# Expert rows added to gathered residual rows per block, in place of a scratch of expert rows and a combine pass

## The reference

```
h = rms_norm(x, g_norm_ffn) * (1 + sc_m) + sh_m
top-1 of 4 groups, then top-2 of the 8 experts inside it      # 2 rows of 32 experts per token
hid = silu(xblk @ w_gate[e]) * (xblk @ w_up[e])               # 1024 -> 256
y[token] += (hid @ w_down[e]) * weight                        # 256 -> 1024
x = x + gt_m * y                                              # gt_m: one row for the prompt, one for the sample
```

## Time and profile before

| what | us |
|---|---|
| median of 3 runs (lowest to highest) | 1254.57 (1252.77 to 1256.62) |
| the profiled execution's own time | 1249.39 |
| its span | 1247.6 |
| TensorE busy in the span | 1070.9 |
| DVE busy | 554.3 |
| ACT busy | 252.5 |
| POOL busy | 186.9 |
| DMA, mean over the span | 200 GB/s |

### The profile page before, as it was taken

One profiled execution on the slowest core, in us unless ns is written; L12 is line 12 of the kernel. 1 busy time (PEld: TensorE's weight loads), 2 busy tenths in 40 slices (PEclk: granted clock), 3 DMA queues, 4 the chain that ended last, 5 costly groups with the idle time before them and its releaser, 6 DMA issues. The chain is left out here.

```text
span 1247.6 us, 13856 instructions
## 1 busy us (share of the span) xinstructions
PE 1070.9 (86%) x4732; PEld 690.1 (55%) x4732; DVE 554.3 (44%) x1110; ACT 252.5 (20%) x595; POOL 186.9 (15%) x267
## 2 busy tenths in 40 slices
PE   4699999999298889989999994399999999999920
PEld 1245555544255455657666753377777777777610
DVE  2345556554363555566575736511222121222147
ACT  1132232222222222332223201011111111111100
POOL 1122222222501101110110000110110011011032
PEclk9799999999677999999999985599999999999975
DMA  8985555441331122221120105649999999999857
GB/s 316 335 304 195 190 189 188 171 154 44 116 88 59 33 78 76 77 93 35 59 74 4 51 34 222 250 155 363 361 375 368 359 371 374 360 363 369 303 193 262
DMA packets 66860, 249.94 MB, mean 200 GB/s; under 512 B 11555, under 2 KB 15286, under 8 KB 51062
## 3 DMA queue, kind: packets, MB, share of 16 engines
q1 hardware_dynamic: 56208, 219.72, 47.5%
q0 software_dynamic: 7216, 26.22, 6.0%
q10 hardware_dynamic: 3382, 3.32, 0.8%
HBM read 195.58 MB, written 53.65 MB: 200 GB/s over the span
## 5 line engine op out<-in xcount | busy, mean ns | idle before, releaser
L903 PE MATMUL bank<-W_in,hT 128*128 128x512 f32 (+3 forms) x432 | 181.3, 573 | 3.4 <-ACTq L1295 3.4
L1061 PE MATMUL bank<-W_out,mT 128*128 128x512 f32 (+1 forms) x288 | 139.7, 618 | 2.9 <-DVEq L1487 2.9
L903 PEld LDWEIGHTS bank<-W_in,hT 128*128 128x128 f32 (+1 forms) x432 | 79.7, 187 | 94.6 <-issue 89.0
L1178 PE MATMUL bank<-WG,xT 128*128 128x256 f32 x528 | 121.3, 383 | 2.4 <-ACT xT L1435 1.9
L1196 PE MATMUL bank<-WD,hidT 128*128 128x512 f32 x264 | 119.0, 593 | 1.6 <-DVE hidT L1961 1.6
L1180 PE MATMUL bank<-WU,xT 128*128 128x256 f32 x528 | 119.3, 379 | 0.0
L1953 DVE TENSOR_TENSOR hid<-sg,bank 128x256 f32<-128x256 f32 x33 | 20.0, 605 | 214.6 <-ACT sg L1442 114.3
L759 POOL TENSOR_SCALAR st<-st 128x1 f32<-128x1 f32 (+6 forms) x77 | 17.7, 230 | 611.9 <-DVEq L1493 611.9
L1180 PEld LDWEIGHTS bank<-WU,xT 128*128 128x128 f32 x528 | 100.3, 190 | 13.6
L1178 PEld LDWEIGHTS bank<-WG,xT 128*128 128x128 f32 x528 | 98.9, 192 | 15.6 <-ACT xT L1435 2.5
L1037 PEld LDWEIGHTS bank<-vall,probT 128*128 128x128 f32 (+1 forms) x656 | 79.2, 190 | 22.0 <-issue 17.9
(11 more groups left out here) (255 smaller groups left out, 1265.8 us busy)
## 6 DMA issues: line engine op xcount, KB each, us to landing
WG<-in_w_gate_e SPq DMA_DIRECT2D x33, 1024.0 KB, 6.0
WU<-in_w_up_e SPq DMA_DIRECT2D x33, 1024.0 KB, 8.0
WD<-in_w_down_e SPq DMA_DIRECT2D x33, 1024.0 KB, 9.7
ada_w<-in_w_ada SPq DMA_DIRECT2D x24, 1024.0 KB, 7.8
expert_rows_scratch<-yb SPq DMA_DIRECT2D x33, 512.0 KB, 3.7
expert_rows_scratch<-zeros SPq DMA_DIRECT2D x8, 1024.0 KB, 11.4
kbuf<-k_scratch SPq DMA_DIRECT2D x12, 384.0 KB, 5.2
xbuf<-in_x_prompt SPq DMA_DIRECT2D x8, 512.0 KB, 3.8
```

What stands on the lines that cost most here:

```text
L903: ins = mm(ps[:R, 0:n], hT[:, t % 2, k, :R], W_in[:, k, c0:c0 + n], start=(k == 0), stop=(k == KD - 1))
L1061: ins = mm(psum[6][:R, :], mT[:, k, :R], W_out[:, k, half * 512:(half + 1) * 512], start=(k == 0), stop=(k == KD - 1))
L1178: mm(psum[2][:, 0:DE], xT[:, k, :], WG[:, slot, k, :], start=(k == 0), stop=(k == KD - 1))
```

## The change

1. The tables carry more. `ids` holds, per slot of a block, the token row, and row numbers for three destinations; a number of 65536 or more marks a slot that takes no part, and the indirect DMAs skip it (`bounds_check`, `oob_is_err=False`). A flag says whether a slot is the first or the second of its token's two rows in the order of blocks. The weights are split into a prompt part and a sample part.
2. Expert blocks are reordered so that neighbouring blocks belong to different groups (block `b` is expert `b % 4 * 8 + b // 4`), and the 33rd block is part of the ordinary loops (`NS = NE + 1`).
3. Per block, ACT computes prompt gate row times weight (`gate_w`, 128x1024), DVE adds sample gate row times weight to it. The output rows are then `yb` = PSUM banks times `gate_w`, both halves on DVE, and `acc` += `yb`, where `acc` holds residual rows that POOL gathered for the block.
4. POOL scatters `acc`: rows of a token's first visit go back to `residual_scratch`, rows of the second visit go to the two outputs. The gather of residual rows for block `b + 1` waits for the scatter to the residual scratch of block `b`.
5. The combine pass, its tiles, the residual loads, the stores of expert rows and the stores of zeros go.

Core of the diff (POOL, ACT, DVE, PE, SP of the expert stage, and the small table operations on DVE):

```diff
 # POOL
+        do(g.memset(xg[:], 0.0))
+        do(g.memset(acc[:], 0.0))
         g.wait_ge(s_tab, 1)
-            do(g.tensor_copy(gi[:, par:par + 1], idx))
-            g.indirect_dma_start(xg[:, par], None, h2_d, bass.IndirectOffsetOnAxis(gi[:, par:par + 1].bitcast(U32), 0)).then_inc(s_xg[par], 16)
+        for b in range(NS):
+            if b + 4 < NS:
+                g.wait_ge(s_xTp, b + 3)
+                tokens(b % 2, at(TOKEN, b + 4))
+            if b:
+                g.wait_ge(s_ysc, 32 * b)
+            g.wait_ge(s_sum, b + 1)
+            first_rows_out(b % 2, at(FIRST, b))
+            last_rows_out(b % 2, at(PROMPT_ROW, b), at(SAMPLE_ROW, b))
+            g.wait_ge(s_zsc, 16 * (b + 1))
+            if b + 1 < NS:
+                rows_in((b + 1) % 2, at(TOKEN, b + 1))
+        g.wait_ge(s_ysc, 32 * NS)
 # ACT
-        def y_half(b, par, nth):
-            act.wait_ge(s_down, b + 1)
-            A(yb[:, par, 0:512], psum[5][:], ACT.Copy, scale=ww).then_inc(s_ya, 1)
+        def gate(b, par, free):
+            if free is not None:
+                act.wait_ge(s_yv, free)
+            A(gate_w[:, par], gate_m[:, 0], ACT.Copy, scale=ww).then_inc(s_gw, 1)
+        with act.Fori(0, (NE - 2) // 2) as i:
+            for u in range(2):
+                b = i * 2 + u
+                silu(b + 1)
+                gate(b + 2, u, i * 4 + (2 * u + 2))
+                xT_half(b + 2)
+        for b in range(NE - 2, NS - 1):
+            silu(b + 1)
+            if b + 2 < NS:
+                gate(b + 2, b % 2, 2 * (b + 1))
+            if b + 2 < NS:
                 xT_half(b + 2)
 # DVE
+        def gate(b, par):
+            dve.wait_ge(s_gw, b + 1)
+            V.scalar_tensor_tensor(gate_w[:, par], gate_m[:, 1], ww, gate_w[:, par], ALU.mult, ALU.add).then_inc(s_gated, 1)
+        def add_rows(b, par, k, nth):
+            dve.wait_ge(s_down, b + 1)
+            for half in range(2):
+                c = slice(half * 512, (half + 1) * 512)
+                V.tensor_tensor(yb[:, c], psum[5 + half][:], gate_w[:, par, c], ALU.mult).then_inc(s_yv, 1)
+            dve.wait_ge(s_yv, b * 2 + 2)
+            dve.wait_ge(s_acc[k], nth)
+            V.tensor_tensor(acc[:, k], acc[:, k], yb[:], ALU.add).then_inc(s_sum, 1)
+        def steady(b, u, nth):
             hidT_(b)
+            gate(b, u % 2)
             hidden(b + 1)
             xT_half(b + 2)
-            y_half(b, b % 2, None)
+            add_rows(b, u % 2, u % 2, nth)
+        # before the one-hot tables, for each of the two rows of a token:
+            do(TT(tokf[:, kk, :], posf[:, kk, :], posf[:, 1 - kk, :], ALU.is_lt))
+            do(V.scalar_tensor_tensor(tokf[:, kk, :], tokf[:, kk, :], FIRST_BIT, tok_id[:], ALU.mult, ALU.add))
+        # after the tables: 5 small operations for the token numbers, signal(s_tab), then 9 more and signal(s_tab)
 # PE
-                pe.wait_ge(s_ya, b)
-                pe.wait_ge(s_yv, b)
+                pe.wait_ge(s_yv, b * 2)
-        for b in range(NE - SLOTS, NE):
+        for b in range(NE - SLOTS, NS):
 # SP
-                store_y(i * SLOTS + u, u % 2)
                 sp.wait_ge(s_down, i * SLOTS + u + 1)
-                load_expert_dyn(i * SLOTS + (SLOTS + u), u)
+                load_expert_dyn(i + (u * EG + 1), u)
-        for t in range(NT + 1):
-            sp.wait_ge(s_yo, t + 1)
-            sp.dma_start(y_rows[t], x2_all[:ROWS[t], t]).then_inc(s_yout, 16)
```

More of the change, by code:

```diff
@@ L46 @@
 NB = NE + MAXOV
-YROWS = NB * P
-ZROWS = MAXOV * P // NT
-assert ZROWS * NT == MAXOV * P and ZROWS % P == 0
+NS = NE + 1
+FAR = 65536.0
+FIRST_BIT = 2048.0
 ADA_PARTS = 4
@@ L308, in build_in @@
     bf = sb("bf", [P, 2, NT + 1])
+    far = sb("far", [P, NB])
+    number = sb("number", [P, NB])
+    first = sb("first", [P, NB])
+    idf = sb("idf", [P, NB])
+    tokf = sb("tokf", [P, 2, NT + 1])
+    assert cursor[0] <= nc.sbuf_usable_end, cursor[0]
     s_params = sem("params_loaded")
@@ L521, in build_in @@
     s_down = sem("down_done")
[L522 to L529, removed]
+    s_gw = sem("prompt_gate_weighted")
+    s_gated = sem("row_gates_ready")
+    s_yv = sem("down_read")
+    s_acc = [sem(f"residual_rows_gathered{i}") for i in range(2)]
+    s_sum = sem("rows_summed")
+    s_zsc = sem("residual_rows_scattered")
+    s_ysc = sem("output_rows_scattered")
+    s_over = sem("overflow_step_passed")
     ctx_block = nc.Block()
@@ L683, in load_expert_dyn @@
             sp.dma_start(WD[:, slot], w["w_down_e"][0, bass.ds(e, 1)].rearrange("o (p k) n -> (o p) k n", k=2)).then_inc(s_wd[slot], 16)
[L685 to L691, removed]
+        for b in range(SLOTS):
+            load_expert(b % NG * EG + b // NG, b)
         sp.wait_ge(s_tab, 1)
@@ L825, in _ @@
[L825 to L832, removed]
+        g.wait_ge(s_rs, n_roots)
+        g.sem_inc(s_end2, 1)
+        g.wait_ge(s_end2, 5)
+        do(g.memset(xg[:], 0.0))
+        do(g.memset(acc[:], 0.0))
+        g.wait_ge(s_tab, 1)
+        U = lambda idx: bass.IndirectOffsetOnAxis(idx.bitcast(U32), 0)
@@ new lines, in _ @@
+        at = lambda kind, b: ids[:, kind, b:b + 1]
+        tokens(0, at(TOKEN, 0))
+        tokens(1, at(TOKEN, 1))
+        rows_in(0, at(TOKEN, 0))
+        for b in (2, 3):
+            g.wait_ge(s_xTp, b - 1)
+            tokens(b % 2, at(TOKEN, b))
+        g.wait_ge(s_tab, 2)
+        for b in range(NS):
[10 more added lines that the diff above has]
+                rows_in((b + 1) % 2, at(TOKEN, b + 1))
@@ L1973, in _ @@
         xT_half(1)
[L1974 removed]
+        def steady(b, u, nth):
             hidT_(b)
+            gate(b, u % 2)
             hidden(b + 1)
             xT_half(b + 2)
[L1978 to L1982 removed]
+            add_rows(b, u % 2, u % 2, nth)
+        for b in range(SLOTS):
+            steady(b, b, 16 * (b // 2 + 1))
+        with dve.Fori(0, (NE - 2 * SLOTS) // SLOTS) as i:
+            for u in range(SLOTS):
+                steady(i * SLOTS + (SLOTS + u), u, i * 32 + (16 * (u // 2) + 48))
+        for b in range(NE - SLOTS, NS):
+            hidT_(b)
+            gate(b, b % 2)
+            if b + 1 < NS:
                 hidden(b + 1)
+            if b + 2 < NS:
                 xT_half(b + 2)
[L1985 to L1990 removed]
+            add_rows(b, b % 2, b % 2, 16 * (b // 2 + 1))
         n_ov = dve.value_load(ovf_i[0:1, MAXOV:MAXOV + 1], min_val=0, max_val=MAXOV)
```

205 lines of the change are left out of this document (80 added, 125 removed).

## The result

The changed kernel takes 1354.47 us at the median of 4 runs (1351.87 to 1367.12), the kernel before 1253.67 (1247.03 to 1256.62). The ratio is 1.083, 95% interval 1.075 to 1.091. The forecast was 1376, 21.5 us too high, inside its range. The profiled execution took 1352.63 us, with a span of 1350.9: 103.3 more than before.

What follows compares the result with a forecast made beforehand. TensorE and DMA were both nearly full, with TensorE pacing blocks at 11.44 us. Start +0.4, stall +110, clock +53, 33rd block -1.4 and end -40.6 gave +121 on 1249.39, 1370.4; plus 5.2 for the median, 1376 us, range 1315 to 1425.

Steps and rivals of the forecast that it cites:

- start, to the first token transposes: Path to the first gather: 1.5 us of added small DVE operations, 1.1 less for POOL's index copy, net +0.4 us.
- from there to the end of down(30), with 30 periods: Expert loop: each block pays 3.55 us of stall and 1.7 us for the clock.
- down(30) to down(32): 33rd block: 18.5 us in place of 19.9, so -1.4 us, beside the stall counted separately.
- end: After the last down projection: gather, add, scatters and landing take 13.1 us in place of 53.7, so -40.6 us.
- ACT's order: Expert loop: xT(b+2) queues behind a gate waiting for block b's products, stalling TensorE 3.55 us per block, 31 blocks, +110 us.
- The clock: Expert loop: TensorE's clock falls after the stall, 1.7 us per block as a mean, +53 us; granted clock 0.8 to 0.9.
- C: Rival: the expert loop stalls without a fall of the clock, 1323 us; 20 in 100.
- D: Rival: every block pays the long clock fall, 31 x 3.0 = 93 us in place of 53, 1416 us; 12 in 100.
- rival B: Expert loop: add, scatter, landing, gather, landing, add sets the period in place of the ACT stall, 1446 us; 10 in 100.
- decides from 7.4 each: Condition for the DRAM chain to set the period: scatter and gather landings of 7.4 us each; forecast 4.0 and 4.6.
- DMA and POOL: Expert loop: weights need 3 MB in 15 us or more, DMA no longer near a bound; POOL's issues take 6.2 of 15.
- A: Rival: the expert loop stays at 11.44 us per block and only the ends change, -41.6, 1213 us; 4 in 100.

Runs made afterwards that it cites:

- e2: Changed kernel with residual rows of block b+1 asked for ahead of block b's scatter, ACT's order unchanged; 1352.7 us, ratio 1.081.
- e7: Changed kernel with ACT's xT copy ahead of the gate and four residual-row buffers, rows asked for two blocks ahead; 1217.95 us, ratio 0.975.
- e8: Changed kernel with the early gather of residual rows, plus three filler matmuls in TensorE's wait for xT; 1320.8 us, ratio 1.056.
- e1: Changed kernel with only ACT's order turned, xT(b+2) ahead of gate(b+2); 1336.5 us, ratio 1.068.
- e9: Four-buffer kernel (e7) with later POOL memsets, the last residual gather waiting for residual scatters alone, and block 32's residual scatter issued last; 1217.2 us, ratio 0.973.
- e6: Kernel with both edits (e3) without the scatter to the sample output, four indirect DMAs per block in place of five; 1272.2 us, ratio 1.019.
- e3: Changed kernel with both edits, xT ahead of the gate on ACT and the early gather of residual rows; 1317.2 us, ratio 1.054.
- e5: Kernel with both edits (e3) with the steady loop's weight loads cut to one eighth; 1219.8 us, ratio 0.975.

## Why the prediction was right, and where its sizes were off

The direction, the mechanism and the bound stood as forecast; the sizes of two terms did not. The account on the profiled execution, predicted +121, measured +103.3:

| part | predicted | measured |
|---|---|---|
| start, to the first token transposes | +0.4 | +5.7 (806.60 to 812.33) |
| from there to the end of down(30), with 30 periods | +157.5 (30 x (3.55 + 1.7)) | +132.4 (367.4 to 499.9) |
| down(30) to down(32) | +3.9 | +0.7 (19.92 to 20.58) |
| end | −40.6 | −35.5 (53.66 to 18.14) |

The sum is nearer than its parts: the loop was forecast 28 us too long, and the start and the end together 10 too short.

*ACT's order.* Right in place and nearly in size. The wait is 3.0 to 3.1 us and a period at full clock is 14.7 to 14.8, so 3.3 per block where I had 3.55: a late matmul start at +3.31 and not +3.53. The two products take 1.29 together where I had 1.41, and the copy of xT starts 0.10 before the row of the gate ends where I had it 0.03 after. All 31 blocks pay it. e2 takes the chain away and changes nothing, e7 takes both away and the period returns to 11.44, so nothing else was in it.

*The clock.* 53 us were taken, 32 were paid. e8 shows the price by the time, and the gate matmuls (156.5 us against 121.3 before) by the trace. The size of one fall was right, 1.69 us (mean period 16.44 against 14.75). The step that failed was to charge it to every block as a mean: 19 of 30 periods are 16.4 to 16.5, the others 14.7 to 14.8, with no fall. Behind waits of 3.02 us, and of 3.10 as well, the clock fell in some blocks and not in others. There is an order in it, in e2 as in the changed kernel: never two short periods one after the other, never more than two long ones. What makes it these traces don't show. Rivals C (none) and D (all, and long) are both refuted by that split. The clock of the stage was 0.93 to 0.94, above the 0.8 to 0.9 that I gave as a sign.

*The chain over DRAM, rival B.* Not the bound, as I said, but by a much smaller margin than I gave. I wrote that DVE does not wait for gathered rows, and that I am wrong if its add waits for a DMA in most blocks. It did, in 24 of 33. By that sign B holds, and it does not: e2 takes 95 us of these waits away and gains nothing. The sign was badly chosen, because a wait on DVE costs only where TensorE waits in turn. I took 10.5 for the chain's length from a scatter of 4.0 and a gather of 4.6; where it sets the pace (e1) it takes 15.4 on average. The second step that failed was this landing. The gather was priced from the first one of the stage and the scatter from row stores of another queue. Measured, a gather issued ahead of the weight loads was used after 4.4 us and one among them after 8.7, and a scatter among them let go after 10.2. The condition "decides from 7.4 each" named the right place: 16 of the 32 scatters let the next gather go later than that, nine gathers were used later than that, and in most blocks only one of the two was slow, so the sum came out even with the stall. That B did not add to the time was luck, and it shows in e1, where undoing the stall gave 18 us of the 136 between the changed kernel and e7.

*The start.* Predicted 0.4, measured 5.7. DVE's small operations were counted rightly (0.8 us more ahead of the table matmuls: 17.76 to 18.58 from one matmul group to the next). Missed were the memset's hold on DVE (1.6, shown by e9), two products of 128x288 that now write in a strided order (0.67 in place of 0.46 each, 0.4), and 2.6 us by which the router matmuls came later already. The change doesn't touch that part of the program, and in the eleven traces of changed kernels the last router matmuls start anywhere between 758.8 and 764.5 us (760.3 before, 762.9 here). So 2.6 us lie within what that part varies from trace to trace, and are not shown to be the change's.

*The end.* Counted from the last down projection: the add began after 4.3 us (predicted 5.05, with a gather of 4.6 that took 3.0) and took 1.23; 0.8 to the first scatter (0.3); three issues of 3.6 in all, where I had counted two, 2.5; and 8.2 from there to the end of the span, where I had 4.0 for a landing. How much of the 8.2 is the landing and how much the program's own end, these rows don't separate.

*DMA and POOL.* Both off the bound, as forecast: DMA share 0.67. But "no longer near a bound" was said of bytes. What came near one was the time of each transfer, and that is not in a share.

The one rival on the other side, A (1213 us), is refuted for this kernel; e7 is a kernel for which it would hold (1218): without the order on ACT and with slack for the chain the change is a gain of 2.5%, and the shorter end is all of it (18.9 us from the last down projection to the end of the span, where it was 53.7).

## What to carry to other kernels

When a wait is found that sets the period, work out the second-longest chain to the same precision and remove both; removing one gives only the distance between them (18 and 2 us here). Both edits together gave 37, because a third wait came up, and the four buffers 136. Ask of a waiting engine whether the bottleneck waits for it; here 95 us of waits on DVE cost nothing. On an in-order engine put the instruction that the bottleneck waits for ahead of one that waits for the bottleneck's result. Count the skipped rows of a small indirect DMA as packets, price its landing by what is in the queues when it is issued, and give such transfers buffers enough to be slow.

## What the runs showed of the hardware

- A row that an indirect DMA skips is still a packet. Leaving out one DMA that moved two rows of 128 took away 144 packets and, with its issue and its landing, 1.4 us per block (e6 against e3).
- A gather of about 68 rows was used 4.4 us after its issue when it was issued ahead of 3 MB of weight loads, and after 8.7 among them; a scatter among them let go after 10.2. With an eighth of the weight bytes the last output scatter of a block let go after 2.9 to 3.5 us, where it took up to 13.4 (e5 against e3). The packets of the weight queue were not fewer in e5, only smaller.
- A POOL memset of 1.80 us stretched a DVE operation on 8 elements per partition from 0.17 to 1.80 us. POOL's issue of a scatter, begun 0.38 us after a DVE operation with two SBUF inputs, took 1.79 in place of 0.99 and ended 0.89 after it, as if it had got going when that operation was done; in e3, where DVE was idle beside it (1015.91), it took 1.01.
- After a wait of 3.0 to 3.1 us TensorE's clock fell to half speed in 19 blocks of 30, never in three running, and never stayed up in two running. Filling 2.7 us of the wait with matmuls kept it at full speed in all of them and was worth 32 us.
